# An overflowing expert's second round: four whole bodies per pair against one body with short branches

## What is computed

```
logits = xt @ router_w + router_b            # xt: 256 tokens x 1024
top_v, top_i = top_k(logits, 4);  gates = softmax(top_v)
for each expert e, over the tokens that chose it:
    gu  = x @ w_gate_up[e] + b_gate_up[e]    # 1024 x 2048: 8.4 MB
    glu, lin = min(gu[:, ::2], 7), clip(gu[:, 1::2], -7, 7)
    act = glu * sigmoid(1.702 * glu) * (lin + 1)
    y   = act @ w_down[e] + b_down[e]        # 1024 x 1024: 4.2 MB
    out[token] += gate * y
```

## Time and profile before

| | us |
|---|---|
| runs | 2752.65, 2752.43, 2746.95 |
| median | 2752.43 |
| the profiled execution | 2747.75 |
| its span in the trace | 2746.0 |
| of which pairs 0 to 15, 317.2 to 1435.9 | 1118.7 |
| pairs 0, 1 and 6 (with a second round) | 99.7, 106.1, 100.7 |
| pairs 8 to 15 together | 499.5 |

### The profile page before, as it was taken

One profiled execution on the slowest core, in us unless ns is written; L12 is line 12 of the kernel. 1 busy time (PEld: TensorE's weight loads), 2 busy tenths in 40 slices (PEclk: granted clock), 3 DMA queues, 4 the chain that ended last, 5 costly groups with the idle time before them and its releaser, 6 DMA issues. The chain is left out here.

```text
span 2746.0 us, 23801 instructions
## 1 busy us (share of the span) xinstructions
PE 2319.6 (84%) x9700; PEld 1338.6 (49%) x9700; DVE 870.6 (32%) x1721; ACT 397.1 (14%) x798; POOL 116.1 (4%) x81
## 2 busy tenths in 40 slices
PE   3978597898878988888877999869779998888998
PEld 2544433233333333333326678646548763546873
DVE  5536321221211221221126525543446401242301
ACT  1021211011101111111102321112121000121100
POOL 1000000000000000000000000000300000000000
PEclk9977697999989999999998999889899999989999
DMA  9542475799978999999977641366225643323441
GB/s 330 204 173 94 187 265 216 286 405 413 414 275 307 382 412 413 405 410 407 381 319 265 245 157 47 113 225 245 92 105 203 214 146 116 123 92 108 153 156 51
DMA packets 213287, 655.72 MB, mean 239 GB/s; under 512 B 8502, under 2 KB 13166, under 8 KB 196548
## 3 DMA queue, kind: packets, MB, share of 16 engines
q1 hardware_dynamic: 209840, 646.11, 62.3%
q0 software_dynamic: 1712, 3.60, 0.4%
q10 hardware_dynamic: 1540, 3.42, 0.3%
HBM read 652.05 MB, written 1.05 MB: 238 GB/s over the span
## 5 line engine op out<-in xcount | busy, mean ns | idle before, releaser
L1351 PE MATMUL ps<-w,XE 128*64 128x512 f32 x1536 | 357.3, 619 | 75.0 <-DMA w<-in_w_gate_up 37.1
L715 PE MATMUL ps<-HF,w 128*128 128x256 f32 x1408 | 311.9, 385 | 1.1 <-ACT HF L688 1.1
L715 PEld LDWEIGHTS ps<-HF,w 128*128 128x128 f32 x1408 | 271.2, 193 | 42.4 <-issue 3.3
L1351 PEld LDWEIGHTS ps<-w,XE 128*64 128x64 f32 x1536 | 122.4, 142 | 299.1 <-issue 299.1
L1376 DVE TENSOR_TENSOR T<-ps,BB 128x512 f32<-128x512 f32 x64 | 44.3, 692 | 571.2 <-PE ps L1351 571.2
L554 DVE SCALAR_TENSOR_TENSOR AUX<-w,CS,AUX 128x512 f32<-128x512 f32 x252 | 189.5, 752 | 9.0
L715 PE MATMUL ps<-HT,w 128*128 128x256 f32 (+1 forms) x656 | 152.8, 392 | 4.8 <-DVE dqk L2028 3.7
L731 PE MATMUL ps<-w,AF 128*128 128x512 f32 x352 | 151.6, 593 | 1.8 <-DVE AF L2620 1.8
L1443 PE MATMUL ps<-GR,AT 128*64 128x512 f32 x256 | 123.6, 640 | 33.4 <-DMA AUX<-in_w_down 31.3
L731 PE MATMUL ps<-w,HT 128*128 128x512 f32 (+1 forms) x352 | 148.0, 576 | 1.1 <-ACT HT L688 1.1
L715 PEld LDWEIGHTS ps<-HT,w 128*128 128x128 f32 (+1 forms) x656 | 126.2, 195 | 26.8 <-issue 6.2
(11 more groups left out here) (553 smaller groups left out, 2592.1 us busy)
## 6 DMA issues: line engine op xcount, KB each, us to landing
w<-in_w_gate_up SPq DMA_DIRECT2D x96, 2048.0 KB, 18.0
w<-in_w_down SPq DMA_DIRECT2D x32, 2048.0 KB, 18.2
w<-in_ada_w SPq DMA_DIRECT2D x24, 2048.0 KB, 7.9
w<-in_ffn_w_in SPq DMA_DIRECT2D x20, 2048.0 KB, 7.9
w<-in_w_in SPq DMA_DIRECT2D x17, 2048.0 KB, 11.0
GR<-in_w_gate_up SPq DMA_DIRECT2D x16, 2048.0 KB, 16.8
AUX<-in_w_gate_up SPq DMA_DIRECT2D x16, 2048.0 KB, 21.5
GR<-in_w_down SPq DMA_DIRECT2D x16, 2048.0 KB, 13.6
```

Source lines behind the costliest of these rows:

```text
L715: ins = e.matmul(out_, w[:, k, c:c + n], HT[:, k, :], start=k == 0, stop=k == kc - 1, skip_group_check=True)
L1351: ins = e.matmul(b[j * n:j * n + n, :], FM.XE[:, side(x, r), 4 * kh + k, j * n:j * n + n], ring.tile(512, 1024, "gu", ex_, h, kh, x[0])[:, ...
```

## The change

Each engine now has one body per pair, and the second round isn't woven into it: `more` puts it at four places on PE (its gather at the start; gate/up of half 0 behind G1b; gate/up of half 1 behind G2b; turns, down and scatter behind D2), four on ACT and four on DVE, at each of them once for each expert (`j`), so eight branches a pair and engine. Its `Else` only waits for the `wide` count and raises it. The flags are now one per expert, and two are loaded per pair. PE's stream has 41,069 instructions after (ACT 2,616 from 3,582, DVE 4,578 from 6,593, SP 718 from 526). A branch skips 74 to 102 PE instructions; where two pairs meet, 368 stand in a row of which about 25 are executed if nobody overflows.

With this: a tile is now left by both, the first round (`pe`, at its last matmul on it) and the second (`wide["pe"]`, in `more_gate_up_pe`/`more_down_pe` or in the `Else` at that place). SP waits for both. The first round's scatter takes its PSUM banks from `gu_bank`. The second round has helper tiles of its own for each `j`. Adding up the sums in `ACCM` is no longer waited for by the next gather.

```diff
-                b = (gu_bank if r else bank2).take(e, x, "sc", t, hf, r)
...
+                b = gu_bank.take(e, x, "sc", t, hf)
...
+    def more_gather_pe(e, x, j):
+        e.wait_ge(*at(x, "pg", j))
...
+    def more_gate_up_pe(e, x, j, h):
+        ex_, row = members(x)[j], slice(32 * j, 32 * j + 1)
+        b = bank2.take(e, x, "gu", h, j)
+        if h == 0:
+            e.wait_ge(*at(x, "xe out", j))
...
+        for kh in range(2):
+            w = ring.tile(512, 1024, "gu", ex_, h, kh, x[0])
+            for k in range(4):
+                for g in range(2):
+                    ins = e.matmul(b[64 * g:64 * g + 64, :], XM(j)[:, 4 * kh + k, :], w[:, k, 512 * g:512 * g + 512], start=False,
+                                   stop=kh == 1 and k == 3, skip_group_check=True)
+        ins.then_inc(*wide["pe"](x, "gu", h, j))
+        for kh in range(2):
+            wide["pe"].leave("w", "gu", ex_, h, kh, x[0])
...
+    def more_down_pe(e, x, j):
+        ex_ = members(x)[j]
+        e.wait_ge(*at(x, "act", 1, j))
+        b = bank2.take(e, x, "turned", "more", j)
+        for i in range(4):
+            ins = e.transpose(b[:, cols(i)], AM(j)[:, cols(i)], ident)
+        ins.then_inc(*wide["pe"](x, "turned", "more", j))
+        b = bank2.take(e, x, "down", "more", j)
+        e.wait_ge(*at(x, "at", "more", j))
...
+        for d in range(2):
+            wide["pe"].leave("w", "down", ex_, d, x[0])
+        e.wait_ge(*at(x, "y", j))
...
+    def more(e, x, over, who, part, *args):
+
+        extra = wide[who]
+        for j in range(2):
+            n, users = extra.n, [list(b.user) for b in (gu_bank, bank2)]
+            with e.If(over[j] == 1):
+                part(e, x, j, *args)
+            with e.Else():
+                if n:
+                    e.wait_ge(extra.sem, n)
+                e.sem_inc(extra.sem, extra.n - n)
+            if who == "pe":
+                for b, user in zip((gu_bank, bank2), users):
+                    b.user = [u + tuple(v for v in w if v not in u) for u, w in zip(user, b.user)]
+
+    def overs(e, x):
+        return [e.value_load(FM.flag[0:1, ex_:ex_ + 1], min_val=0, max_val=1) for ex_ in members(x)]
+
+
+
+    def pair_pe(e, x):
         p = x[1]
-        for r in rounds[1:]:
-            gather_pe(e, x, wide["pe"], r)
-        gate_up_pe(e, x, 0, 0, rounds)
-        gate_up_pe(e, x, 0, 1, rounds)
+        over = overs(e, x)
+        more(e, x, over, "pe", more_gather_pe)
+        gate_up_pe(e, x, 0, 0)
+        gate_up_pe(e, x, 0, 1)
+        more(e, x, over, "pe", more_gate_up_pe, 0)
         between_pe(e, p)
-        gate_up_pe(e, x, 1, 0, rounds)
-        for r in rounds:
-            expert_turn_pe(e, x, 0, r)
-        gate_up_pe(e, x, 1, 1, rounds)
-        down_pe(e, x, 0, range(3), rounds)
-        for r in reversed(rounds):
-            expert_turn_pe(e, x, 1, r)
-        down_pe(e, x, 0, range(3, 4), rounds)
-        down_pe(e, x, 1, range(4), rounds)
-        for r in rounds[1:]:
-            scatter_pe(e, x, r)
+        gate_up_pe(e, x, 1, 0)
+        expert_turn_pe(e, x, 0)
+        gate_up_pe(e, x, 1, 1)
+        more(e, x, over, "pe", more_gate_up_pe, 1)
+        down_pe(e, x, 0, range(3))
+        expert_turn_pe(e, x, 1)
+        down_pe(e, x, 0, range(3, 4))
+        down_pe(e, x, 1, range(4))
+        more(e, x, over, "pe", more_down_pe)
 
...
+    def pair_act(e, x):
         p = x[1]
+        over = overs(e, x)
+        more(e, x, over, "act", more_gather_act)
+        gate_up_act(e, x, 0)
+        gate_up_act(e, x, 1)
+        more(e, x, over, "act", gate_up_more_act, 0)
         if p + 1 < len(PAIRS):
+            gather_act(e, PAIRS[p + 1])
+        expert_turn_act(e, x, 0)
+        gate_up_act(e, x, 2)
+        gate_up_act(e, x, 3)
+        more(e, x, over, "act", gate_up_more_act, 1)
+        expert_turn_act(e, x, 1)
+        down_act(e, x)
+        more(e, x, over, "act", more_down_act)
+
+    def gate_up_more_act(e, x, j, h):
+        gate_up_act(e, x, h, j)
+
+    def pair_dve(e, x):
         p = x[1]
+        over = overs(e, x)
+        e.wait_ge(*at(x, "pg turned"))
+        more(e, x, over, "dve", more_gather_dve)
         if p + 1 < len(PAIRS):
+            gather_dve(e, PAIRS[p + 1])
+        gate_up_dve(e, x, 0)
+        gate_up_dve(e, x, 1)
+        more(e, x, over, "dve", more_gate_up_dve, 0)
         before_dve(e, p)
+        gate_up_dve(e, x, 2)
+        gate_up_dve(e, x, 3)
+        more(e, x, over, "dve", more_gate_up_dve, 1)
+        more(e, x, over, "dve", scatter_dve)
 
...
-    def pair(e, x, body, tally, who):
...
-        p = x[1]
-        either = e.value_load(FM.flag[0:1, p:p + 1], min_val=0, max_val=1)
-        with e.If(either == 1):
-            both = e.value_load(FM.flag[0:1, 17 + p:18 + p], min_val=0, max_val=1)
-            with e.If(both == 1):
-                way("both", (0, 1))
-            with e.Else():
-                first = e.value_load(FM.flag[0:1, 33 + p:34 + p], min_val=0, max_val=1)
-                with e.If(first == 1):
-                    way("a", (0, "a"))
-                with e.Else():
-                    way("b", (0, "b"))
-        with e.Else():
-            way("", (0,))
-        assert len(set(counts)) == 1
-        extra.n = n2 + max(used)
-        for b, all_users in zip((gu_bank, bank2), users):
-            b.user = all_users
-
```

More of the change, by code:

```diff
@@ L1204, in members, with side @@
         return (2 * x[1], 2 * x[1] + 1) if x[0] == "pair" else (x[1],)
-    def side(x, r):
-        return 2 if r else x[1] % 2 if x[0] == "pair" else 0
+    def side(x):
+        return x[1] % 2 if x[0] == "pair" else 0
     def before(x, n=1):
@@ L1238, in bias_pool @@
     def bias_pool(e, x):
-        after(e, before(x), "act", 3, 0)
+        after(e, before(x), "act", 3)
         e.wait_ge(*at(x, "rows"))
@@ L1276, in gather_pe @@
[L1276 to L1286, removed]
+            e.tensor_scalar(PG[:, 0, t, :], iota, 128.0, FM.rk[:, t, es[0]:es[0] + 1], ADD, ALU.is_equal).then_inc(*dve())
@@ L1287, in gather_pe @@
+            own(e, dve)
+            e.tensor_scalar(PG[:, 1, t, :], PG[:, 0, t, :], FM.G[:, t, es[0]:es[0] + 1], None, MUL).then_inc(*dve(x, "pg"))
+    def gather_pe(e, x):
+        e.wait_ge(*at(x, "pg"))
+        for k in range(0, 8, 4):
+            b = bank2.take(e, x, "xe", k)
             for j in range(4):
@@ new lines, in expert_turn_pe, with expert_turn_act @@
+    def expert_turn_pe(e, x, d):
+        e.wait_ge(*at(x, "act", 2 * d + 1))
+        b = bank2.take(e, x, "turned", d)
+        for j in range(4):
+            ins = e.transpose(b[:, cols(j)], A_[:, cols(4 * d + j)], ident)
+        ins.then_inc(*pe(x, "turned", d))
+    def expert_turn_act(e, x, d):
+        if d == 0:
+            after(e, before(x), "down", 1)
+        e.wait_ge(*at(x, "turned", d))
+        e.activation(FM.AT[:, 4 * d:4 * d + 4, :].rearrange("p k n -> p (k n)"), bank(x, "turned", d), ACT.Copy).then_inc(
+            *act(x, "at", d))
+        act.leave("bank", x, "turned", d)
@@ new lines, in more_gate_up_dve @@
+    def more_gate_up_dve(e, x, j, h):
+        own(e, dve)
+        own(e, wide["dve"])
+        e.wait_ge(*at(x, "gu", h, j))
+        clamped_dve(e, bank(x, "gu", h, j).rearrange("p (n a) -> p n a", a=2), wide["dve"], x, (h, j),
+                    AM(j)[:, 256 * h:256 * h + 256], (x, "gu", h, j))
+    def more_down_pe(e, x, j):
[8 more added lines that the diff above has]
+        for d in range(2):
+            w = ring.tile(512, 1024, "down", ex_, d, x[0])
+            for k in range(4):
+                for g in range(2):
+                    ins = e.matmul(b[64 * g:64 * g + 64, :], FM.XE[:, 2, 4 * d + 2 * j + k % 2, 64 * (k // 2):64 * (k // 2) + 64],
+                                   w[:, k, 512 * g:512 * g + 512], start=d == 0 and k == 0, stop=d == 1 and k == 3,
+                                   skip_group_check=True)
+        ins.then_inc(*wide["pe"](x, "down", "more", j))
+        for d in range(2):
+            wide["pe"].leave("w", "down", ex_, d, x[0])
+        e.wait_ge(*at(x, "y", j))
+        for t in range(2):
+            for hf in range(2):
+                b, rows = bank2.take(e, x, "sc", j, t, hf), slice(64 * hf, 64 * hf + 64)
+                e.matmul(b, FM.PGT[rows, 2 + j, cols(t)], AM(j)[rows, :], start=True, stop=True,
+                         skip_group_check=True).then_inc(*wide["pe"](x, "sc", j, t, hf))
```

443 lines of the change are left out of this document (171 added, 272 removed).

## The result

The changed kernel takes 2706.52 us (median of four, 2701.68 to 2711.11), the one before 2752.54 beside it: a ratio of 0.9846, 95% interval 0.9821 to 0.9871. A second set on another occasion gave 0.9854 (0.9822 to 0.9885). That is faster by 46 us.

What follows compares the result with a forecast made beforehand. DMA at 412 GB/s bounds pairs without overflow; overflowing pairs are a chain from freed slots to matmuls, with far-jump stalls. Terms -11 - 4 + 4 = -11 us gave 2740 us, range 2724 to 2764.

Steps and rivals of the forecast that it cites:

- the signs that I named: Expected in the profile after: PEq waits, pair 0 and 6 lengths, pair 6's D2 wait, idle DMA stretches, steady pairs' rate.
- A: Rival: slots held too long starve the queue in pairs without overflow, about +2 us each, 2759; chance 0.23.
- D: Rival: the stalls at 434.16 and 785.44 were waits for VectorE's gather and stay, 2750; chance 0.08.
- part 2: Overflowing pairs: the second round comes in one piece, same TensorE work, but its tiles are given back later.
- the recurrence: Step-by-step timing of pairs 0 to 2, 6 and 7 from step durations and which earlier step's slots each fetch takes.
- my -11: Forecast change of the whole time in us: -11 (pairs 6, 7), -4 (pairs 0 to 2), +4 (eleven others).
- Part 3's +4: Eleven other pairs: slots also wait for the Else's count and free later; +0.4 us each, +4 in all.
- The reserve that I had worked out as nil: Steady pairs, D2's and G1b's slots: 22.6 us left from release to use, 23.8 wanted if one step stands ahead.
- the leap hides there: In pairs bound by DMA a leap costs nothing, since G1b's weights are waited for right behind it.
- rival B's mechanism: Leaps also cost in steady pairs: -1.5 to -2 us for 11 pairs on top of -11, 2720; chance 0.07.
- those that I let pair 0 gain by its branches and lose again: Pair 0: gains 3 us, its branches having cost 3.83 at L1621, and loses them again.
- Rival C: Short branches in a row stall too, 2.7 us each at overflowing pairs and the seam behind; 2747; chance 0.12.

Runs made afterwards that it cites:

- fixed_count: after_fixed with the Else's count kept on PE, no branches, so tiles come free as late as in the changed kernel: 2697.02 us, ratio 0.9809.
- after_step: Changed kernel, but both experts' tiles of a step are left only behind the branches of both experts: 2743.63 us, ratio 0.9983.
- after_swap: Changed kernel with the two experts' branches in the other order on all three engines: 2739.93 us, ratio 0.9968.
- after_fixed: Changed kernel with second rounds placed at build time, without flags, branches or Else counts in the pairs: 2696.74 us, ratio 0.9817.
- before_fixed: Kernel of before with each pair's body chosen at build on PE, ACT and DVE, no branches or flag loads: 2686.0 us, ratio 0.9769.
- fixed_leap: before_fixed plus one never-taken block of 2,727 PE instructions at each pair's head, plain code behind it: 2705.71 us, ratio 0.9848.
- after_leap: Changed kernel plus one never-executed block of 2,727 PE instructions at each pair's head, short branches behind it: 2793.15 us, ratio 1.0156.

## Why the prediction was right or wrong

**Direction and cause: right.** The far jumps were the loss, pairs 1, 2, 6 and 7 the main place, and a short branch costs little, 0.21 us where I had taken 0.08. Of the signs that I named, no wait for PEq is over 3 us (2.4), pair 6 is below 95 us, and the eleven steady pairs are in the mean 0.5 us shorter than before; they move 406 to 407 GB/s in the long windows of pairs 3 to 5 and 8 to 14, where before moved 412 and 405. Three signs failed. Pair 6's D2 waited 1.55 us and not 5, and DMA's idle stretches in pairs 1 and 6 are under 6 us and not 12 to 20; both point to the step below (pair 0, where no tile comes early, has one of 13 us ahead of its D2). Pair 0 is shorter than 99.7, for another reason (see below): its overflowing expert is the first one, whose tile SP wants first. Rivals A and D fell, A by fixed_count, D by L1439 no longer waiting for PEq.

**The size: wrong, by one step above all.** The step is in part 2, "G1a and G1b both become free behind the second round's half", and in the recurrence's rule for slots. It is so only for the overflowing expert's tile. The other's is given back by its own Else, and in pairs 1 and 6 that comes first. The diff showed it: `more` runs its branches one expert after the other, and `more_gate_up_pe` leaves only `ex_`'s tiles. I carried the steps as units of two tiles because the code before leaves them so. The kernel for which my rule is true is after_step. The term was worth 37 us (2743.6 against 2706.5), 33 by after_swap, of the 35 by which my -11 missed. For after_step itself the recurrence gave -11, and it stands 4 us (ratio 0.9983) below before by its times. Its pair 6's D2 waits 6.86 us, forecast 5.6. But that the sums lie so near is in part luck. The recurrence gave 99.1, 59.0, 91.1 and 59.1 us for pairs 1, 2, 6 and 7, together 17 less than after_step's 325.6. It had pair 0 too long by some 6 us, and the eleven others, put at +4, are 5 us shorter than before.

**Part 3's +4 was nothing that shows.** fixed_count against after_fixed: 0.3 us. The reserve that I had worked out as nil sufficed.

**Steady pairs.** I said that the leap hides there behind G1b's wait. It hid in part: before's eight last pairs are 1.3 us each longer than before_fixed's, and 0.7 of it comes with one leap on PE alone (fixed_leap). That was rival B's mechanism, at a lower price. The changed kernel got back 0.4 of it in pairs 8 to 15 (499.5 to 496.5), for the branches and loads of flags cost 7.0 us there (489.5 in after_fixed).

**Pair 0.** I forecast 422.3 for its end, it was 416.1. I had given its gather half clock, as before has it behind 4.54 us of idle time (first row). With 0.96 us ahead of it the gather took 3.79 us, at the full 2.4 GHz (granted clock 1.00; second row, after). That is 3.3 us; the other 3 are those that I let pair 0 gain by its branches and lose again, and it didn't lose them:

```profile
321.79 7.06 PE L1282 MATMUL ps<-PG,XN 128*128 128x64 f32 x32 [4.54 <-issue]
```

```profile
318.26 3.79 PE L1439 MATMUL ps<-PG,XN 128*128 128x64 f32 x32 [0.96 <-DVE PG L1430]
```

The wait of 4.42 us ahead of pair 1's gather came as forecast (4.5), and the gather then took 6.51 us, most of it at half clock (granted clock 0.50 from 422 to 427).

**Rival C was half right.** Stalls do come at the seam, in 7 of 128 places. After_fixed and fixed_count put the whole cost of branches and flags at 8 to 10 us. That this is the seam's stalls in the main and not the 0.2 us of each branch is argued from their records, not shown: PE itself waited for PEq only 7.5 us in this trace and 3.0 in the second set's.

## What to carry to other kernels

A branch costs by where it lands, not by itself. In this kernel skips of 74 to 102 PE instructions cost 0.21 us except at the seams; from 128 on a stall of 3.5 us or more came with the skip or in the branches right behind it (one execution, most lengths once), and from 448 on the leap itself cost 6 to 7. So keep what a sequencer skips well under 128 instructions, and above all don't let one skip follow another before plain code has been run. Where a transfer waits for a buffer, count releases tile by tile in the order in which the code gives them, and ask which of them the queue wants first. A woven order by short branches had both advantages here (2692.5 us), and gives most of what bodies chosen at build give (2686.0).

## What was not expected of the hardware

Two stalls in a row cost far more than twice one: a leap with plain code behind it cost 0.7 us in a steady pair (fixed_leap), one followed by a stalled short branch 7.5 us (after_leap). That the first uses up the sequencer's lead is my explanation; no run varies the lead. A leap's price doesn't grow with its length: 6.28 us for 448 instructions, 6.04 for 4096. But it differs with the place: in fixed_leap the one at pair 0, while DMA is at a share of 0.02, takes 3.34 us, and the fifteen others, with weights on the way (1.02 in the two looked at), 5.8 to 6.3. That the busy DMA is the reason is not tested.
